# A two-block layer kernel: gate rows and the S5 gelu moved from their own stages into the second block's input projection

## The reference, cut to what matters

```python
a = rms_norm_2(h, ln_mix_pre[l])
proj = a @ w_in[l]
y_a = s5_mixer(s5_u, ...)         # the part whose end moves
y_c = fox_mixer(fox_q, fox_k, fox_v, fox_f + gb[0:4], ...)
y_d = mlstm_mixer(ml_q, ml_k, ml_v, ml_o, ml_i + gb[4:8], ml_f + gb[8:12], ...)
# in s5_mixer, after the scan over the sequence:
y = (einsum(x_re, c_re) - einsum(x_im, c_im)) + d_skip * uf
g = jax.nn.gelu(y)
y = g * jax.nn.sigmoid(g @ w_glu)
# in fox_mixer and mlstm_mixer: running sums over time of log_sigmoid of the gates,
# and for mLSTM a running maximum
cum_logf = jnp.cumsum(jax.nn.log_sigmoid(fz), axis=1)
```

## Time and profile before

| | us |
|---|---|
| timed runs, median of 3 | 1804.71 (1803.56 to 1804.91) |
| profiled execution, its own time | 1806.47 |
| profiled execution, span of its instructions | 1804.6 |
| mean granted PE clock over the span | 0.911 |

### The profile page before, as it was taken

The page is one execution under the profiler, slowest core; times in us unless marked ns, Lnnn a source line. Parts: engine busy times, 40 slices in busy tenths (PEclk is TensorE's granted clock), DMA queues, the critical chain, the costliest instruction groups (busy, mean ns, idle before and its releaser), DMA issues. The chain is left out here.

```text
span 1804.6 us, 18401 instructions
## 1 busy us (share of the span) xinstructions
PE 1625.3 (90%) x7372; PEld 1303.4 (72%) x7372; DVE 827.6 (46%) x1217; ACT 554.9 (31%) x839; POOL 260.4 (14%) x275
## 2 busy tenths in 40 slices
PE   7987999668989899999998999399976899999997
PEld 6875777556767788888876667355775688888886
DVE  4233333456655444443454762463674543323334
ACT  4222333424443422232334212334122422212222
POOL 0000000000022795000011763000220200000000
PEclk9998999789999999999998999655568999999999
DMA  4322121220022222222222211100001123222222
GB/s 165 104 76 73 47 71 36 71 71 1 1 82 77 87 97 105 102 94 93 94 93 79 70 70 66 36 23 1 1 1 53 64 97 107 100 94 94 94 82 94
DMA packets 34633, 129.23 MB, mean 72 GB/s; under 512 B 4548, under 2 KB 18780, under 8 KB 22132
## 3 DMA queue, kind: packets, MB, share of 16 engines
q1 hardware_dynamic: 34260, 127.93, 20.6%
q10 hardware_dynamic: 288, 0.12, 0.0%
HBM read 124.82 MB, written 3.17 MB: 71 GB/s over the span
## 5 line engine op out<-in xcount | busy, mean ns | idle before, releaser
L223 DVE TENSOR_TENSOR ring_lo<-ring_raw,ring_hi 128x2048 fp32r<-128x2048 f32 (+5 forms) x115 | 267.7, 2331 | 246.3 <-ACT ring_hi L213 246.2
L242 PE MATMUL bank<-xT_hi,ring_hi 128*128 128x512 f32 (+1 forms) x864 | 343.7, 398 | 5.1 <-PEq L1257 3.4
L242 PE MATMUL bank<-xT_hi,ring_lo 128*128 128x512 f32 (+1 forms) x864 | 340.0, 393 | 0.0
L242 PE MATMUL bank<-xT_lo,ring_hi 128*128 128x512 f32 (+1 forms) x864 | 339.8, 393 | 0.0
L213 ACT CAST ring_hi<-ring_raw 128x2048 fp32r<-128x2048 f32 (+5 forms) x115 | 213.0, 1854 | 274.7 <-DMA ring_raw<-in_w_ff 130.8
L242 PEld LDWEIGHTS bank<-xT_hi,ring_hi 128*128 128x128 f32 (+1 forms) x864 | 164.0, 190 | 45.1 <-issue 10.0
L242 PEld LDWEIGHTS bank<-xT_hi,ring_lo 128*128 128x128 f32 (+1 forms) x864 | 163.3, 189 | 35.9
L242 PEld LDWEIGHTS bank<-xT_lo,ring_hi 128*128 128x128 f32 (+1 forms) x864 | 163.8, 190 | 34.3
L242 PE MATMUL bank<-ring_hi,hid_hi 128*128 128x512 f32 x432 | 169.9, 393 | 3.8 <-DVE ring_lo L223 3.8
L242 PE MATMUL bank<-ring_lo,hid_hi 128*128 128x512 f32 x432 | 169.4, 392 | 0.0
L242 PE MATMUL bank<-ring_hi,hid_lo 128*128 128x512 f32 x432 | 169.2, 392 | 0.0
(11 more groups left out here) (440 smaller groups left out, 2305.1 us busy)
## 6 DMA issues: line engine op xcount, KB each, us to landing
ring_raw<-in_w_ff SPq DMA_DIRECT2D x32, 1024.0 KB, 4.9
ring_raw<-in_w_up SPq DMA_DIRECT2D x22, 1024.0 KB, 4.9
ring_raw<-in_w_proj SPq DMA_DIRECT2D x8, 1024.0 KB, 5.1
ring_raw<-in_w_gates SPq DMA_DIRECT2D x8, 1024.0 KB, 4.9
ring_raw<-in_w_out SPq DMA_DIRECT2D x8, 1024.0 KB, 4.9
ring_raw<-in_w_fm SPq DMA_DIRECT2D x12, 512.0 KB, 4.3
ring_raw<-in_w_dn_a SPq DMA_DIRECT2D x6, 1024.0 KB, 4.9
ring_raw<-in_w_proj SPq DMA_DIRECT2D x8, 512.0 KB, 4.6
```

Source lines behind the costliest of these rows:

```text
L223: k.nc.vector.tensor_tensor(k.ring.lo[:, g % SLOTS, 0:n], k.raw[:, g % SLOTS, 0:n], plain(k.ring.hi[:, g % SLOTS, 0:n]), ALU.subtract).the ...
L242: mm = k.nc.tensor.matmul(out, x, y, start=first and n == 0, stop=last and n == 3 * len(pairs) - 1)
```

## The change

The two stages `stage_gate_rows` and `stage_s5_gelu` go; their operations become methods of two classes, and `stage_proj2` calls these at places in its engines' lists. The bodies of the computation are the same except for buffers' addresses, the banks (the gate transposes in banks 4 and 5, the gate product in 6 and 7) and the counts of semaphores. `project(6)` and `project(7)` stand one chunk earlier, each inside its chunk. On PE the order of the products and the transposes of the gelu is swapped. "..." stands for code that is left out or the same as in the functions above.

```diff
 def second_block(k, out):
-    g, yS = stage_proj2(k, g)
     k.ycat = k.sb("ycat", 16, [P, T, D])
-    stage_gate_rows(k)
-    g = stage_s5_gelu(k, yS, g)
+    g = stage_proj2(k, g)
     stage_fox(k)
 def stage_proj2(k, g):
+    rows, glu = GateRows(k), S5Glu(k, end)
+    j_tg = j_tm + 2 * T
         def _(sp):
-            issue_chunks(k, sp, end + SLOTS)
+            issue_chunks(k, sp, end + SLOTS - 2)
+            rows.sync(sp)
+            issue_chunks(k, sp, end + 1 + SLOTS)
+            rows.arrived(sp)
         def _(pe):
...
-                    if 0 <= n - 2 < 8:
+                    if 0 <= n - 2 < 6:
                         project(n - 2)
                     if 0 <= n < 8:
                         inject(n)
                     wait_chunk(k, pe, c)
+                if (c, j) == (first + 9, j_tm + 1):
+                    project(6)
+                if (c, j) == (first + 10, j_tm + T + 2):
+                    project(7)
+                if (c, j) == (first + 11, j_tm + T + 2):
+                    rows.turn(pe)
+                if j == j_tg + 2:
+                    rows.read(pe)
+                    glu.turn(pe)
...
+            glu.products(pe)
         def _(act):
             for j in range(n_tiles):
                 split_hi(k, act, fin[j] + LEAD)
                 act.wait_ge(done.sem, done.base + j + 1)
                 copy(act, j).then_inc(copied.sem, 1)
+                if j == j_tm + T - 1:
+                    rows.logs(act)
+                if j == j_tm + T + 2:
+                    rows.limits(act)
+                    glu.logistic(act)
+                if j == j_tg:
+                    glu.high_part(act)
                 split_hi(k, act, fin[j] + LEAD + 1)
             split_hi(k, act, end + LEAD)
+            glu.gates(act)
         def _(dve):
             for n in range(8):
                 unit(n)
                 split_lo(k, dve, first + n + LEAD + 3)
-            split_lo(k, dve, end + LEAD - 1)
+            dve.wait_ge(out_done.sem, out_done.base + 7)
+            rows.small(dve)
+            rows.sums(dve)
+            split_lo(k, dve, end)
             dve.wait_ge(out_done.sem, out_done.base + 8)
-            for f in range(2):
-                v.scalar_tensor_tensor(out=yS[:, f, :], ...)
+            glu.cube(dve, uT)
+            rows.keep(dve)
+            split_lo(k, dve, end + 1)
+            glu.weigh(dve)
+            glu.low_part(dve)
             split_lo(k, dve, end + LEAD)
+            glu.scale(dve)
         def _(pool):
...
+            pool.wait_ge(out_done.sem, out_done.base + 7)
+            rows.fill(pool)
-def stage_s5_gelu(k, yS, g):
-def stage_gate_rows(k):
+class S5Glu:
+    def cube(self, dve, u):       # yS from banks 6 and 7, then its square, its factor, its cube
...
+        v.tensor_tensor(t1[:, :, :], t1[:, :, :], yS[:, :, :], ALU.mult).then_inc(self.cubed.sem, 1)
+    def logistic(self, act):
+        act.wait_ge(self.cubed.sem, self.cubed.base + 1)
...
+    def weigh(self, dve):
+        dve.wait_ge(self.sigmoid.sem, self.sigmoid.base + 1)
...
+    def high_part(self, act):
+        act.wait_ge(self.gelu.sem, self.gelu.base + 1)
...
+    def low_part(self, dve):
+        dve.wait_ge(self.high.sem, self.high.base + 1)
...
+    def turn(self, pe):           # the eight transposes of the gelu, banks 4 and 5
+        pe.wait_ge(self.gelu.sem, self.gelu.base + 1)
...
+    def products(self, pe):
+        pe.wait_ge(self.low.sem, self.low.base + 1)
+        wait_chunk(k, pe, g)
+        for t in range(T):
+            products(k, self.out(t), [(self.gs[:, f, t * P:(t + 1) * P], slot(k, g, f * 256, f * 256 + 256))
+                                      for f in range(2)], True, True).then_inc(self.free.sem, 1)
+    def gates(self, act):
+        for t in range(T):
+            act.wait_ge(self.free.sem, self.free.base + 2 * (t // 2) + 2)
+            self.k.nc.scalar.activation(self.sgd[:, t, :], self.out(t), ACT.Sigmoid).then_inc(self.gate.sem, 1)
+    def scale(self, dve):
+        dve.wait_ge(self.turned.sem, self.turned.base + 1)
+        for t in range(T):
+            dve.wait_ge(self.gate.sem, self.gate.base + t + 1)
+            k.nc.vector.tensor_tensor(k.ycat[:, t, 0:256], self.sgd[:, t, :], ..., ALU.mult)
+class GateRows:
+    def sync(self, sp):           # the six small transfers
+        sp.wait_ge(self.split.sem, self.split.base + 2)
+        sp.wait_ge(self.ones.sem, self.ones.base + 3)
...
+    def arrived(self, sp):
+        sp.wait_ge(self.moved.sem, self.moved.base + 16 * 6)
+    def fill(self, pool):         # three memsets
...
+    def logs(self, act):          # Exp, then Ln
+        act.wait_ge(self.low.sem, self.low.base + 1)
...
+    def small(self, dve):         # memset, two tensor_scalar, one tensor_tensor
...
+        v.tensor_tensor(e, e, z, ALU.min).then_inc(self.low.sem, 1)
+    def sums(self, dve):          # scans and splits; raises made, then split twice
+        dve.wait_ge(self.log.sem, self.log.base + 2)
...
+    def turn(self, pe):           # eight transposes, banks 4 and 5
+        pe.wait_ge(self.made.sem, self.made.base + 1)
...
+    def keep(self, dve):          # acol
+        dve.wait_ge(self.turned.sem, self.turned.base + 1)
...
+    def limits(self, act):        # mcol
+        act.wait_ge(self.turned.sem, self.turned.base + 1)
...
+    def read(self, pe):
+        pe.wait_ge(self.turned.sem, self.turned.base + 3)
```

More of the change, by code:

```diff
@@ L1891, in stage_proj2 @@
     bufs = [k.sb("s5_a0", 166, [P, 4, S]), k.sb("s5_a1", 138, [P, 4, S])]
-    yS = k.sb("s5_yS", 164, [P, 2, S])
     uT = fm[:, 0:2, :]
@@ L2018, in _ @@
                 split_lo(k, dve, first + n + LEAD + 3)
-            split_lo(k, dve, end + LEAD - 1)
+            dve.wait_ge(out_done.sem, out_done.base + 7)
+            rows.small(dve)
+            rows.sums(dve)
+            split_lo(k, dve, end)
             dve.wait_ge(out_done.sem, out_done.base + 8)
-            for f in range(2):
-                v.scalar_tensor_tensor(out=yS[:, f, :], in0=uT[:, f, :], scalar=col(k, "s5_d", f),
-                                       in1=k.pb[6 + f][:, :], op0=ALU.mult, op1=ALU.add)
+            glu.cube(dve, uT)
[3 more added lines that the diff above has]
+            glu.low_part(dve)
             split_lo(k, dve, end + LEAD)
+            glu.scale(dve)
         @block.gpsimd
@@ L2039, in _ @@
                 tt(e_i, e_i, e_r, ALU.add).then_inc(prod.sem, 1)
+            pool.wait_ge(out_done.sem, out_done.base + 7)
+            rows.fill(pool)
+    rows.close()
+    glu.close()
     for s in (bu, taken, scanned, prod, out_done):
@@ L2043, in stage_proj2 @@
     copied.base += n_tiles
-    return end, yS
-def stage_s5_gelu(k, yS, g):
[L2049 to L2114, removed]
@@ L2117, in stage_gate_rows @@
-def stage_gate_rows(k):
[L2122 to L2175, removed]
-            link(v.tensor_tensor(R[2], grow[0:4, 1, :], e[0:4, 0, :], ALU.subtract))
-            link(v.tensor_tensor_scan(e[0:4, 1, :], R[2], zz, 0.0, ALU.max, ALU.max))
-            v.tensor_scalar(R[3], e[0:4, 1, :], -1.0, None, ALU.mult)
-            link(v.tensor_tensor(e[0:4, 1, :], e[0:4, 1, :], e[0:4, 0, :], ALU.add))
-            v.tensor_scalar(R[4], e[0:4, 1, :], -1.0, None, ALU.mult).then_inc(hand.sem, 1)
-            for i, row in enumerate((0, 1, 3)):
-                x = v.tensor_copy(parts[i][0:4, 0, :], R[row])
-            x.then_inc(split.sem, 1)
-            dve.wait_ge(split.sem, split.base + 1)
-            for i, row in enumerate((0, 1, 3)):
-                x = v.tensor_tensor(parts[i][0:4, 1, :], R[row], plain(parts[i][0:4, 0, :]), ALU.subtract)
-            x.then_inc(split.sem, 1)
-            dve.wait_ge(hand.sem, hand.base + 5)
-            nc.vector.tensor_copy(k.acol[:, :, :].rearrange("p t h -> p (t h)"), k.pb[0][:, 0:16])
-        @block.gpsimd
-        def _(pool):
-            for dst in (k.f_left, k.f_right, k.m_row):
-                nc.gpsimd.memset(plain(dst[:, :]), 1.0).then_inc(ones.sem, 1)
-        @block.tensor
-        def _(pe):
-            pe.wait_ge(hand.sem, hand.base + 4)
-            for t in range(T):
-                nc.tensor.transpose(k.pb[0][:, 4 * t:4 * t + 4], rows[0:4, 2, t * P:(t + 1) * P], k.ident[0:4, 0:4])
-                mm = nc.tensor.transpose(k.pb[1][:, 4 * t:4 * t + 4], rows[0:4, 4, t * P:(t + 1) * P],
-                                         k.ident[0:4, 0:4])
-            mm.then_inc(hand.sem, 1)
-    hand.base += 5
-    moved.base += 16 * 6
-    ones.base += 3
-    split.base += 2
@@ new lines, in stage_proj2, with __init__, out, close @@
+    return end + 1
+class S5Glu:
+    def __init__(self, k, g):
+        self.k, self.g = k, g
+        self.yS = k.sb("s5_yS", 164, [P, 2, S])
+        self.t1 = k.sb("s5_g1", 200, [P, 2, S])
+        self.gT = k.sb("s5_gT", 190, [P, 2, S])
+        self.gs = k.split("s5_g", 194, [P, 2, S], 104)
+        self.sgd = k.sb("s5_sg", 186, [P, T, 256])
```

(54 more changed lines are left out.)

66 lines of the change are left out of this document (added).

## The result

The changed kernel takes 1773.77 us, the median of 4 runs (1772.77 to 1774.64), against 1804.81 (4 runs, 1803.56 to 1808.32): ratio 0.9827, 95% interval 0.9815 to 0.9839, or 31.0 us less. The forecast was 1773.0 within 1767 to 1779. The profiled execution took 1772.93, its span is 1771.1.

A forecast was written before the change was run, and what follows sets the result against it. PE bounds the kernel, busy 90% of the span, with a hole before FoX. FoX's start moves from 1174.51 to 1142.77 after PE's added work and tail: 31.7 us gained, 1773.0 us forecast, range 1767 to 1779.

The forecast's parts named there:

- The hole goes as a whole: Between the projection's last matmul and FoX's first: all 38.20 us go, then PE's added work and the tail are added back.
- PE's own share: Added to PE's list in the projection: gate transposes 1.00 us, gelu transposes 1.04, 24 gate products 2.88.
- The tail behind PE: From PE's last matmul to FoX: sigmoids 0.78 us, last DVE product 0.36, way to FoX 0.30, two handovers 0.10.
- The chain keeps up: DVE and ACT work in chunks 9 to 12: every result ready before PE asks, smallest slacks 1.6, 2.5 and 2.9 us.
- POOL: Eighth unit beside `rows.small` on DVE: no hindrance taken; at the bound it ends 3.6 us later and PE waits 1.2.
- The clock: Full through the gate products; its fall in FoX and later rises could shift the time 1.7 us to either side.
- Rival 1: FoX keeps the full clock, entered from dense matmuls; about 15 us of its 61.5 saved, 1758 us; chance 0.07.
- Rivals 2 and 3: PE waits mid-chunk, some 6 us come back, 1779 us, chance 0.08; or rows so late that the time is 1806.
- Rival 3: Rows so late that PE stands at `rows.turn`, with half clock after some 4 us idling; time 1806 us; chance 0.01.
- Rival 4: The stage's end waits for something else, say SP's `rows.arrived`, so most of the hole stays; 1804 us; chance 0.02.
- The S5 products' new place: `project(6)` and `project(7)` inside chunks 9 and 10: only change places, 1.83 us each before and after, slacks 1.6 and 2.5.

## Why the prediction was right, point by point

- **The hole goes as a whole.** Right: FoX 54.60 us after the last S5 unit's start, forecast 1142.77 - 1087.77 = 55.00.
- **PE's own share.** A little too dear: the gate transposes take 0.58 us (1116.57 to 1117.15) instead of the 1.00 of half clock, the gelu's 0.8 instead of 1.04. Of these 0.7 us about 0.3 came back in restarts of the dense row, which the sum had left out, such as the matmul of 0.50 behind the gate transposes. The 24 products at 0.12 held.
- **The tail behind PE.** Forecast 1.54, measured 1.50 (1138.15 to 1139.65). The allowance of 0.05 for a handover was a guess: from PE's last matmul to the sigmoid it was 0.03 (1138.15 to 1138.18).
- **The chain keeps up.** In us from the last S5 unit's start: rows made at 25.6 forecast, 25.9 measured; asked for at 31.4, 31.5; gelu made at 40.9, 40.9; asked for at 43.8, 43.4. The slacks were real: a delay of 4 us cost nothing, one of 8 us cost 2.5 of waiting.
- **POOL.** The mis-sized term. I took no hindrance, since only one of the four DVE operations has two inputs, and kept 3.6 us as the bound; it was 1.8, and the operations with one input hindered too, so the reason was wrong. Of the slack of 2.5 there 0.8 was left, so it stayed hidden. That nothing came of it is luck in the forecast: by its own bound PE would have waited. Had the product stood one tile earlier it would have cost 1.9, as the run shows.
- **The clock.** The full clock held to the end of the gate products. The ground given for it, that nothing lets it fall while PE is dense, isn't a rule: behind a wait of 2.5 us it fell with PE at work. In FoX it fell 2 us sooner than before, inside the margin taken for it, and the rest grew by 1.36, within the 1.7 allowed to either side.
- **Rival 1**, FoX at full clock, fell: its clock was 0.50 in the 62 us from 1142 on.
- **Rivals 2 and 3** didn't come true, but the runs with delay show their price. Rival 3 counted the clock's loss only after some 4 us of idling; in one run 2.5 us of waiting brought it. The 1.9 us of the earlier product, also one run, cost none.
- **Rival 4** didn't come true: the six small transfers were issued by 1117.3, long before the stage's end.
- **The S5 products' new place** was costed at nothing, and is worth nothing.

The sum was right in the stretch (31.7 forecast, 32.1 measured, the two errors of PE's share partly cancelling). In the timed runs it is 31.0, the same within their interval of 29.1 to 33.4; 32.1 less the 1.36 of the rest would be 30.8.

## What to carry to other kernels

When a serial chain of small DVE and ACT work stands between two dense stages of PE, its worth is the hole less PE's own share, and whether moving it works is read from one list: when each result is made, and when PE asks for it in its order. Keep such a list with the slack of each wait; here the smallest, 0.8 us, stood where two engines hinder each other and no number of before showed it. A wait inside a dense row can cost more than itself, since the clock may fall after PE is back at work: here one of 2.5 us did and one of 1.9 didn't, a single run each, which sets no limit between them.

## What the runs showed that I had not expected

- In a run each: a wait of 2.5 us in a dense row cost 4.2 us: the clock fell 1.4 us after PE had resumed and stayed at half for 3.4 us. A wait of 1.9 us cost 1.9, one of 6.3 cost 8.4.
- DVE operations on four partitions hinder POOL as those on 128 do, and are hindered: 5.6 us instead of 3.6 for the four, 1.8 us later for POOL.
- The stage's end cost 1.3 us of PE even when a mere copy of 0.37 us trailed the last matmul.
